# Two layer norms in a row (the last of one block, the first of the next) computed from one set of token sums

## What is computed

```python
def first_block(x, ...):
    for l in range(DEPTH):
        ...
        x = layer_norm(ALPHA * x + mix, ln1_g[l], ln1_b[l])
        ffn = conv_ffn(x, w_up[l], ffn_conv_w[l], ffn_conv_b[l], w_down[l])
        x = layer_norm(ALPHA * x + ffn, ln2_g[l], ln2_b[l])
    return x

def second_block(x, ...):
    h = layer_norm_2(x, ln0_g, ln0_b)
    for i in range(DEPTH):
        u = h @ w_in[i]
        ...
```

## Time and profile before

| | us |
|---|---|
| median of 3 runs | 2755.15 (2754.2 to 2760.44) |
| the profiled execution: its own time | 2753.57 |
| its span in the profile | 2751.8 |
| TensorE busy | 2691.8 (98%) |
| granted TensorE clock, mean | 0.987 of full |

### The profile page before, as it was taken

How to read it: one execution, slowest core, us unless ns; L and a number is a source line. 1 busy time by engine, 2 the same in 40 slices (tenths; PEclk the granted TensorE clock), 3 DMA queues, 4 the chain that set the end, 5 groups by cost and what they waited for, 6 DMA issues and landing times. The chain is left out here.

```text
span 2751.8 us, 35283 instructions
## 1 busy us (share of the span) xinstructions
PE 2691.8 (98%) x12370; PEld 2103.7 (76%) x12370; DVE 1719.8 (62%) x2512; ACT 1100.0 (40%) x1901; POOL 1599.7 (58%) x985
## 2 busy tenths in 40 slices
PE   8999999999999999999999999999999999999998
PEld 6777778888887777788888877778766677787775
DVE  6787755444127787654442138876777588777775
ACT  3744423222025544332221031644555415545554
POOL 5754476666676744486666665576236564772253
PEclk9999999999999999999999979999999999999999
DMA  4322222333322322223333322226796222257951
GB/s 156 92 77 62 69 85 77 99 97 94 99 85 85 101 69 62 70 79 98 99 92 99 104 78 85 77 92 240 297 354 218 69 92 77 92 209 284 350 189 65
DMA packets 89530, 338.21 MB, mean 123 GB/s; under 512 B 21552, under 2 KB 24368, under 8 KB 80048
## 3 DMA queue, kind: packets, MB, share of 16 engines
q1 hardware_dynamic: 66592, 298.02, 32.4%
q0 software_dynamic: 19008, 26.28, 3.7%
q10 hardware_dynamic: 3792, 12.06, 1.2%
HBM read 366.67 MB, written 33.55 MB: 145 GB/s over the span
## 5 line engine op out<-in xcount | busy, mean ns | idle before, releaser
L184 POOL TENSOR_TENSOR wl<-ring,wh 128x1024 fp32r<-128x1024 f32 x317 | 781.1, 2464 | 26.5
L182 POOL TENSOR_SCALAR wh<-ring 128x1024 fp32r<-128x1024 f32 x317 | 350.0, 1104 | 726.2 <-PE ps L261 508.0
L259 PE MATMUL ps<-xh,wh 128*128 128x512 f32 x1592 | 633.4, 398 | 13.5 <-DVE xl L1272 10.7
L261 PE MATMUL ps<-xh,wl 128*128 128x512 f32 x1592 | 621.2, 390 | 0.0
L260 PE MATMUL ps<-xl,wh 128*128 128x512 f32 x1592 | 621.0, 390 | 0.0
L259 PEld LDWEIGHTS ps<-xh,wh 128*128 128x128 f32 x1592 | 299.3, 188 | 94.5 <-issue 12.6
L261 PEld LDWEIGHTS ps<-xh,wl 128*128 128x128 f32 x1592 | 299.3, 188 | 63.7
L260 PEld LDWEIGHTS ps<-xl,wh 128*128 128x128 f32 x1592 | 299.7, 188 | 61.0 <-issue 1.0
L1519 DVE SCALAR_TENSOR_TENSOR taps<-ps,par,taps 128x511 f32<-128x511 f32 x192 | 143.9, 749 | 232.2 <-ACT taps L1246 217.3
L3118 DVE TENSOR_TENSOR ew_l<-ew,ew_h 128x1024 fp32r<-128x1024 f32 x184 | 214.1, 1218 | 7.4 <-ACT ew_h L2641 7.4
L2641 ACT ACTIVATE ew_h<-ew 128x1024 fp32r<-128x1024 f32 x184 | 180.7, 1050 | 14.8 <-DMA ew<-in_eu 11.4
(11 more groups left out here) (556 smaller groups left out, 5309.0 us busy)
## 6 DMA issues: line engine op xcount, KB each, us to landing
ring<-in_w SPq DMA_DIRECT2D x343, 512.0 KB, 3.6
ew<-in_eu SPq DMA_DIRECT2D x32, 2048.0 KB, 12.3
ew<-in_ed SPq DMA_DIRECT2D x32, 1024.0 KB, 11.6
xrows<-xr ACTq DMA_DIRECT2D x8, 512.0 KB, 2.7
yrows<-xr ACTq DMA_DIRECT2D x8, 512.0 KB, 3.7
yg<-yrows SPq DMA_DIRECT2D x8, 512.0 KB, 5.3
z<-in_x SPq DMA_DIRECT2D x4, 512.0 KB, 5.6
out<-z SPq DMA_DIRECT2D x8, 256.0 KB, 2.9
```

What stands on the lines that cost most here:

```text
L182: nc.gpsimd.tensor_scalar(hi, raw, 1.0, 0.0, ALU.mult, ALU.add).then_inc(sem["w_hi"], 1)
L184: nc.gpsimd.tensor_tensor(lo, raw, hi, ALU.subtract).then_inc(sem["w_split"], 1)
L259: nc.tensor.matmul(out, wh, xh, start=first, stop=False, **kw)
L261: return nc.tensor.matmul(out, wl, xh, start=False, stop=last, **kw)
```

## The change

The second norm of a normalised row can be had without making that row. If z is the sum before the first norm, with mean and reciprocal root of its own, then mean and variance of the second norm follow from six sums over the channels of each token: of z; of z weighted by the gain, by its square, and by gain times centred shift; of z²; and of z² weighted by the gain's square. So the new kernel

- lets DVE accumulate three weighted sums of the tiles beside the down products (`acc`, L542 and L543), ACT make a second, weighted square of each tile (L643), and DVE add these (`sqg`, L547);
- lets DVE prepare constants out of rows of gains and shifts (`prepare`, L557 to L601), loaded by a new 2 MB transfer that ACT issues (`low["rows"]`, L1359);
- puts 20 token-sum matmuls on PE ahead of the very last down unit (`weighted`), and 12 behind it (`sums`);
- drops both passes over z in the first block, the second round of squares and sums, and the barrier now comes behind a chain of small instructions (`statistics`, L608 to L633), which leaves four rows for each token;
- makes the norm in the second block as z·gain·scale + shift (L684, L690 on DVE), where scale and shift come out of PE matmuls of 14 rows (L669, L672, and one `shift_rows` matmul for each chunk, L665), three of them ahead of the products and five between them; ACT then only copies to `xh` (L699).

```diff
+        join = (("col", 184.75, [P, 40], F32), ("gains", 185, [P, C8], F32), ("parts", 185.25, [P, 4, J_ROWS], F32),
+                ("high", 186, [P, 4, JOIN], F32R), ("four", 185.5, [P, 4, JOIN], F32), ("stat", 185.75, [P, 13, 4], F32),
+                ("of_rows", 192, [P, D], F32R), ("rows", 196, [P, S], F32R), ("of_scale", 198, [P, P], F32R))
+        self.join = {name: mem.at("join_" + name, kb, shape, dt)[tuple(slice(None) for _ in shape)] for name, kb, shape, dt in join}
...
+        if ahead is not None:
+            ahead(pe, i)
...
+def joined_sums(nc, sem, sh, r, norm, z0, ident, ones_d, eps, sqb, sqa, za, low, gain, gains, shifts):
+    ps, z, tile = sh.ps, sh.z, sh.join
+    ps_sum, ps_sq = ps[:, 7, 0:16].rearrange("p (j w) -> p j w", w=JOIN), ps[:, 5, 0:8].rearrange("p (j w) -> p j w", w=2)
+    acc, sqg, sqg_in, scratch, rows = (low[n] for n in ("acc", "sqg", "sqg_in", "scratch", "rows"))
+    high_rows, low_rows = low["high_rows"], low["low_rows"]
+    g1r, b1r, g2r, b2r = (rows[:, n, :] for n in range(4))
+    col = tile["col"]
+    w2, wb, rz, rs, means, mean_b, eps2 = col[:, 0:8], col[:, 8:16], col[:, 16:20], col[:, 20:22], col[:, 22:26], col[:, 26:27], col[:, 27:28]
+    own, is_low, is_high, is_b2, is_r, minus = col[:, 28:32], col[:, 32:33], col[:, 33:34], col[:, 34:35], col[:, 35:36], col[:, 36:37]
+    stat = tile["stat"]
+    sums, four = stat[:, 0:4, :], tile["four"]
+    dd, n1, nn, t, n3, var, std, r1, v = (stat[:, n, :] for n in range(4, 13))
...
+        def token_sums(self, out, src, w, cols, first=False, last=False):
+            for j in range(4):
+                mm = nc.tensor.matmul(out[:, j, w:w + cols.shape[-1]], src[:, j * P:j * P + P], cols, start=first and j == 0, stop=last,
+                                      skip_group_check=True)
+            return mm
+        def weighted(self, pe):
+            pe.wait_ge(sem["weighted"], 1)
+            for n in range(3):
+                self.token_sums(ps_sum, acc[:, n, :], n + 1, ones_d[:, 0:1], n == 0)
+            self.token_sums(ps_sq, sqg, 1, ones_d[:, 0:1], True)
+            pe.wait_ge(sem["sq_acc"], (r + 1) * (C8 - 2))
+            self.token_sums(ps_sq, sqa, 0, ones_d[:, 0:1])
         def sums(self, pe):
+            pe.wait_ge(sem["za_ready"], r + 1)
+            self.token_sums(ps_sum, za, 0, ones_d[:, 0:1])
+            pe.wait_ge(sem["z_ready"], z0 + C8)
+            self.token_sums(ps_sum, z[:, C8 - 1, :], 0, rz, last=True).then_inc(sem["sum_mm"], 1)
             pe.wait_ge(sem["sq_part"], (r + 1) * C8)
+            self.token_sums(ps_sq, sqb[:, (C8 - 1) % 2, :], 0, rs, last=True).then_inc(sem["sqs_mm"], 1)
...
+        def add(self, dve, do, m, bank):
             V = nc.vector
+            norm[1].add(dve, do, m, bank)
+            if m == 0 or m == C8 - 1:
+                return
+            for n, weight in enumerate((gains, w2, wb)):
+                if m == 1:
+                    do(V.tensor_scalar(acc[:, n, :], z[:, 0, :], weight[:, 0:1], None, ALU.mult))
+                do(V.scalar_tensor_tensor(acc[:, n, :], z[:, m, :], weight[:, m:m + 1], acc[:, n, :], ALU.mult, ALU.add))
+            for k in range(m - 1, m + 1 if m == C8 - 2 else m):
+                if k:
+                    dve.wait_ge(sem["wsq_part"], k + 1)
+                    V.tensor_tensor(sqg, sqg_in[:, 0, :] if k == 1 else sqg, sqg_in[:, k % 2, :], ALU.add).then_inc(sem["wsq_acc"], 1)
+                    dve.wait_ge(sem["wsq_acc"], k)
+            if m == C8 - 2:
+                dve.sem_inc(sem["weighted"], 1)
+        def prepare(self, dve, do, m):
...
+            if m == 0:
+                dve.wait_ge(sem["rows_in"], 16)
+                do(V.reduce_sum(mean_b, b1r, AXX))
+                do(V.tensor_scalar(mean_b, mean_b, 1.0 / D, None, ALU.mult))
+                do(V.scalar_tensor_tensor(w2, gains, 2.0, gains, ALU.mult, ALU.mult))
+                do(V.tensor_scalar(wb, shifts, mean_b, 2.0, ALU.subtract, ALU.mult))
+                do(V.tensor_tensor(wb, wb, gains, ALU.mult))
+                do(V.tensor_copy(rz[:, 0:1], ones_d[:, 0:1]))
+                for n, weight in enumerate((gains, w2, wb)):
+                    do(V.tensor_scalar(rz[:, n + 1:n + 2], weight[:, C8 - 1:C8], 1.0 / D, None, ALU.mult))
+                do(V.tensor_copy(rs[:, 0:1], ones_d[:, 0:1]))
+                do(V.tensor_scalar(rs[:, 1:2], rz[:, 2:3], 0.5, None, ALU.mult))
+            elif m == 1:
+                do(V.tensor_scalar(b1r, b1r, mean_b, None, ALU.subtract))
+                do(V.reduce_sum(means[:, 0:1], g1r, AXX))
+                do(V.tensor_tensor(scratch, g1r, g1r, ALU.mult))
...
+            elif m == 3:
+                one = lambda n: ident[:, n:n + 1]
+                do(V.reduce_sum(own.unsqueeze(2), ident[:, 0:3 * JOIN].rearrange("p (g q) -> p q g", q=JOIN), AXX))
+                do(V.reduce_sum(is_low, ident[:, JOIN:2 * JOIN], AXX))
+                do(V.tensor_tensor(is_low, is_low, one(J_ROWS - 1), ALU.add))
+                do(V.reduce_sum(is_high, ident[:, 0:J_ROWS], AXX))
+                do(V.tensor_tensor(is_high, is_high, is_low, ALU.subtract))
+                do(V.tensor_tensor(is_b2, one(J_ROWS - 2), one(J_ROWS - 1), ALU.add))
+                do(V.tensor_tensor(is_r, one(JOIN - 1), one(3 * JOIN - 1), ALU.add))
+                do(V.tensor_scalar(minus, own[:, 2:3], -1.0, None, ALU.mult))
+                do(V.tensor_scalar(scratch, g1r, minus, own[:, 1:2], ALU.mult, ALU.add))
+                do(V.scalar_tensor_tensor(scratch, b1r, own[:, 0:1], scratch, ALU.mult, ALU.add))
+                do(V.tensor_tensor(scratch, scratch, g2r, ALU.mult))
+                do(V.scalar_tensor_tensor(scratch, b2r, is_b2, scratch, ALU.mult, ALU.add))
+            elif m == 4:
...
+                do(V.tensor_tensor(low_rows, scratch, high_rows, ALU.subtract))
+                do(V.tensor_scalar(high_rows, high_rows, is_high, None, ALU.mult))
+                do(V.scalar_tensor_tensor(tile["of_rows"], low_rows, is_low, high_rows, ALU.mult, ALU.add))
...
+            delta, a1, a2, ab = (sums[:, j, :] for j in range(4))
             dve.wait_ge(sem["sum_mm"], r + 1)
+            do(V.tensor_copy(sums, ps_sum.rearrange("p j w -> p w j")))
+            do(V.tensor_tensor(dd, delta, delta, ALU.mult))
+            do(V.scalar_tensor_tensor(n1, delta, means[:, 0:1], a1, ALU.mult, ALU.subtract))
+            do(V.tensor_tensor(nn, n1, n1, ALU.mult))
+            do(V.scalar_tensor_tensor(t, delta, means[:, 1:2], a2, ALU.mult, ALU.subtract))
             dve.wait_ge(sem["sqs_mm"], r + 1)
+            V.tensor_tensor(var, ps_sq[:, :, 0], dd, ALU.subtract).then_inc(sem["var_ready"], 1)
+            do(V.tensor_tensor(t, t, delta, ALU.mult))
+            do(V.tensor_tensor(v, ps_sq[:, :, 1], nn, ALU.subtract))
+            do(V.tensor_tensor(v, v, t, ALU.add))
+            do(V.scalar_tensor_tensor(n3, delta, means[:, 2:3], ab, ALU.mult, ALU.subtract))
             dve.wait_ge(sem["std_there"], r + 1)
+            do(V.reciprocal(r1, std))
+            do(V.tensor_tensor(v, r1, v, ALU.mult))
+            do(V.tensor_tensor(v, v, n3, ALU.subtract))
+            V.tensor_tensor(var, v, r1, ALU.mult).then_inc(sem["var_ready"], 1)
+            dve.wait_ge(sem["std_there"], r + 2)
+            do(V.reciprocal(four[:, :, 0], std))
+            do(V.tensor_tensor(four[:, :, 3], four[:, :, 0], r1, ALU.mult))
+            do(V.tensor_tensor(four[:, :, 1], four[:, :, 3], n1, ALU.mult))
+            do(V.tensor_tensor(four[:, :, 2], four[:, :, 3], delta, ALU.mult))
+            parts, high = tile["parts"], tile["high"]
+            do(V.tensor_scalar(high, four, 1.0, None, ALU.mult))
+            do(V.tensor_copy(parts[:, :, 0:2 * JOIN].rearrange("p j (d q) -> p j d q", q=JOIN),
+                             high.unsqueeze(2).to_broadcast([P, 4, 2, JOIN])))
+            do(V.tensor_tensor(parts[:, :, 2 * JOIN:3 * JOIN], four, high, ALU.subtract))
...
+            norm[2].squares(act, m)
+            if m < C8 - 1:
+                if m > 1:
+                    act.wait_ge(sem["wsq_acc"], max(m - 2, 1))
+                nc.scalar.activation(sqg_in[:, m % 2, :], z[:, m, :], ACT.Square, scale=gain(m)).then_inc(sem["wsq_part"], 1)
...
+def joined_rows(nc, sem, sh, ident):
+    ps, z, xh, xl, tile = sh.ps, sh.z, sh.xh, sh.xl, sh.join
+    ps_rows, ps_scale = ps[0:J_ROWS, 4, :], ps[:, 5, :]
+    rows = tile["rows"][0:J_ROWS, :]
+    def shift_rows(pe, k):
+        if k >= 4:
+            pe.wait_ge(sem["xa_ready"], k - 3)
+        nc.tensor.matmul(ps[:, k % 4, :], tile["of_rows"][0:J_ROWS, k * P:k * P + P], rows, start=True, stop=True).then_inc(sem["in_shift"], 1)
     def tensor(pe):
         for j in range(4):
+            mm = nc.tensor.transpose(ps_rows[:, j * P:j * P + P], tile["parts"][:, j, :], ident)
+        mm.then_inc(sem["in_turned"], 1)
+        pe.wait_ge(sem["in_copied"], 1)
```

(49 more changed lines are left out.)

139 lines of the change are left out of this document (45 added, 94 removed).

## The result

The changed kernel takes 2771.55 us (median of 6 runs, 2765.12 to 2774.14) against 2756.98 us for the kernel before (6 runs, 2750.84 to 2760.44). The ratio is 1.005, with a 95% interval of 1.0038 to 1.0061: slower by 0.4 to 0.6%, that is by 10.5 to 16.8 us, where no change was forecast (2754.8, range 2748 to 2760). The profiled execution took 2771.33 us, its span 2769.4.

What follows compares the result with a forecast made beforehand. PE, busy 98% of the span, was taken as the bound, with a 30.5 us seam between blocks. Terms -13.9 + 4.5 + 5.5 + 1.5 + 1.1 + 1.0 = -0.3 gave 2754.8 us as median, range 2748 to 2760.

Steps and rivals of the forecast that it cites:

- A: Block's end, last unit to end of `statistics`: shorter chain, some instructions held by POOL, ends 13.9 us earlier.
- B: 20 weighted sums on PE ahead of the last down unit: five groups of four, paid in full, +4.5 us.
- C: Down tiles: DVE's two-SBUF-input instructions wait for POOL, late additions make PE wait; +5.5 us, bounds 0 and +11.5.
- the stepping: Tile-by-tile reckoning of DVE and POOL delays in the down tiles: PE waits 2.7 and 3.1 us in tiles 5 and 6.
- D: Head of the second block: about 4.95 us to the first product against 3.44, +1.5 us.
- E: Five shift matmuls between the second block's first products: 5 x 0.227, +1.1 us.
- F: Last down unit: clock may fall during the weighted sums; price 0 or 2 to 2.6, taken as +1.0 us.
- Rival 2: Down tiles: late squares hold POOL's splits, over 0.2% slower if C reaches 11.3; 2760.8 us with 11.5; chance 0.15.

Runs made afterwards that it cites:

- e10: As e9, with the small instructions of `statistics` taking one of their two operands from PSUM: 2747.4 us, ratio 0.9959.
- e9: As e7, with the 20 weighted sums issued three at a time behind each of the last down unit's chunks: 2747.94 us, ratio 0.9965.
- e3: Changed kernel with VectorE's preparation instructions dealt out otherwise, the first to tile 0, the others in small pieces to tiles 1 to 6: 2763.45 us, ratio 1.0023.
- e4: Changed kernel with two of the three weighted sums kept in PSUM until tile 6: 2761.63 us, ratio 1.0011.
- e1: Changed kernel with all nine token-row matmuls on 128 rows instead of 14, the added rows being zeros: 2763.16 us, ratio 1.0025.
- e2: Changed kernel without the five shift matmuls between the products, part of the shift left out: 2761.51 us, ratio 1.0015.
- e7: Changed kernel with the edits of e1, e3 and e4 together: 2753.36 us, ratio 0.998.
- e12: The changed kernel, unchanged, profiled once more: 2766.64 us.
- e8: As e7, with the 20 weighted sums issued behind the last down unit instead of ahead of it: 2747.4 us, ratio 0.9953.

## Why the prediction was wrong

*A, end of the block (-13.9): right.* The end came 10.8 us behind the last unit, 11.2 forecast, and -14.3 against the old one. The held instructions are the forecast ones, but one came through: the fourth, `nn`, starts at 1624.46, 0.04 before GpSimd's next split, and takes 0.16. The fifth was held in its place, for 2.20, to 0.02 behind that split's end (1626.84). e10 shows the cause to be the SBUF inputs. (Two counts of sums are wrong ahead of the result, and no term rests on them: the 13.8 us of L498 are 32 sums, which leave 64 records, and "36 sums" behind the last unit are 56 by the order shown there.)

*B, 20 sums (+4.5): right.* In e9, at full clock, sums and unit take 10.0 us, the unit alone 5.44: 4.6.

*C, down tiles (+5.5): mechanism right, size short.* PE waited 5.9 us in three places (0.85, 3.80, 1.23, tiles 4 to 6), where the stepping had two, 2.7 and 3.1, in tiles 5 and 6. VectorE's additions of tiles 3, 4 and 5 start at 1542.62, 1563.08 and 1582.51, the middle one some 8 us behind PE's last product of its tile (1554.97). Two things weren't in the sum. From start to start the three waits cost 6.7 us, since a matmul that waits doesn't overlap the one before. And behind the one of 3.8 us the clock fell, 0.83 in 1570 to 1580, which is 1.7 us. That makes 8.4 of the measured +8.5, 3.0 more than forecast. e3 and e4 each remove it.

*D, head (+1.5): right*, +1.35.

*E, five shift matmuls (+1.1): the step that failed.* "5 x 0.227 = +1.1" takes the spacing of products, with 128 rows, for instructions that have 14, and the sum left the clock's return behind the first product where it was in the old trace. With 128 rows (e1 less e2) the price is 1.0, as forecast. With 14 rows the stretch is 7.65 us longer in the first trace, and 28.7 to 29.1 us long instead of 19.17 in the three others, 9.6 to 9.9 more: at least 6.5 us above the term, the largest miss and alone more than the 0.2% that the runs can tell. A part is each matmul's own price at the low clock: 1.87 us for three steps instead of 1.28. The rest is the clock, which stays at 1.2 GHz until the last of them, and in three of the four traces some 5 us longer. That it could be late at the head was in neither the sum nor a rival. Why it stays, whether through the few rows or through the weight loads that no longer start ahead, is not shown.

*F, clock in the last unit (+1.0): mis-sized.* Sums and unit took 13.3 us instead of 10.0: +3.3. The same order took 11.5 in e7, 11.6 in e12, 13.2 in e3 and e4 and 14.9 in e1 and e2, so the term varies from 1.5 to 4.9 between executions, and the upper end of 2.6 was too low.

Sum of the measured terms in the first trace: -14.3 + 4.6 + 8.5 + 1.35 + 7.65 + 3.3 = +11.1, less 0.2 at tile 1 the +10.8 seen at the emb matmul. It lies 11.4 above the forecast sum of -0.3; E has 6.5 of that, C 3.0 and F 2.3. E's miss alone puts the forecast at 2761.3, and those of C and F together put it at 2760.1, each just past the range's end; E's is the largest, and the one for which the prediction had no bound at all. The medians differ by 14.6, with an interval from 10.5 to 16.8 us; the first trace's 10.8 lies at its lower end, and what the medians have beyond it is in part the longer head of the other traces and otherwise not attributed. Rival 2 (slower through C of 11.3 or more) had the right sign and, with C at 8.5, not the cause.

## What to carry to other kernels

A matmul with few rows among products isn't priced by its columns: here zeros up to full height gave the clock back 10 us or more earlier. Ask of every thin stretch (sums of one column, few rows) where the clock stands behind it, not only what it costs itself. Deal one-column sums out between products. A side job on VectorE with two SBUF inputs is priced with its waits for GpSimd's running instruction: put one operand in PSUM, and put the job where the engine is idle, since lateness adds up from tile to tile. With these the shortened seam did pay: ratios of 0.9953 to 0.9965 (e8 to e10) instead of 1.005. Before comparing two traces of one pair, take a second trace of each kernel: here the head varied by 2 us, the last unit by 3 and the later stages by 8.

## Not expected of the hardware

- TensorE without a gap for 10 us (1640 to 1650), 14-row matmuls among its products, kept the low level of 1.2 GHz, in four traces for 16 to 21 us; with zeros up to 128 rows it was at 2.4 GHz 3.8 to 6.1 us behind the first product in five.
- The weights of a 14-row matmul, and those of the product behind it, were loaded only when their matmuls started; with 128 rows the load started 0.43 us ahead.
- Three steps from start to start around a 14-row matmul take 1.87 us at the low clock, around one with 128 rows 1.28 (1639.18 to 1640.46).
- GpSimd's splits (means of 1521 to 1590) were lengthened from 2415 and 1049 ns to 2675 and 1304 beside VectorE's work in e3, and that alone cost nothing: PE had no wait for a split.
- A small VectorE instruction with two SBUF inputs that started 0.04 us before GpSimd's next split took 0.16 us; its neighbours, which started inside one, ended with it.
- Short falls of the clock in the later stages mostly recur at the same places, but which of them fall changes between executions of one kernel: 5.1 and 13.6 us in total in two of the changed one.
